# First products of the key/value compression: three rounded passes over two sequences at once, page rows in another order

## What is computed

```python
def compress(kv, pe, w1, w2):                      # kv: (B, L, 2, groups, 64)
    nch = L // 16                                  # 64 chunks of 16 rows
    ch = kv.reshape(B, nch, 16, 2, 2, 64)
    h = einsum('cld,cldh->ch', pe, w1b)            # position term
    for r in range(2):                             # a window is 32 rows: two chunks
        u = einsum('bnscgd,csdh->bncgh', ch, w1r[:, r])
        h = h + u[:, r:r + nch - 1]
    return einsum('bncgh,chd->bncgd', gelu(h), w2)
```

## Time and profile before

| | |
|---|---|
| median of 3 runs | 2172.89 us (2168.56 to 2173.81) |
| profiled execution | 2165.8 us |
| span of its profile, first to last instruction | 2164.2 us |
| mean granted TensorE clock | 0.918 of full |
| busy share PE / PEld / DVE / ACT / POOL | 87% / 73% / 49% / 39% / 9% |

### The profile page before, as it was taken

One profiled execution on the slowest core, in us unless ns is written; L12 is line 12 of the kernel. 1 busy time (PEld: TensorE's weight loads), 2 busy tenths in 40 slices (PEclk: granted clock), 3 DMA queues, 4 the chain that ended last, 5 costly groups with the idle time before them and its releaser, 6 DMA issues. The chain is left out here.

```text
span 2164.2 us, 26795 instructions
## 1 busy us (share of the span) xinstructions
PE 1879.3 (87%) x9820; PEld 1589.7 (73%) x9820; DVE 1059.8 (49%) x1953; ACT 841.7 (39%) x1706; POOL 186.4 (9%) x336
## 2 busy tenths in 40 slices
PE   5996975678888997959948997799999999999997
PEld 4895863457667775738737872699998999989996
DVE  3532345536777875455334441454445544455444
ACT  4311222225666665232034531443333433344443
POOL 0001102103333321010000000000000000000000
PEclk8998987776899998969968998799999999999999
DMA  5414404210000002140022002434333433344341
GB/s 189 182 37 104 115 1 126 89 37 1 1 1 1 1 1 73 54 163 8 1 90 78 1 16 82 137 125 142 122 116 135 162 123 117 119 161 157 138 154 63
DMA packets 109977, 185.21 MB, mean 86 GB/s; under 512 B 18416, under 2 KB 79280, under 8 KB 109799
## 3 DMA queue, kind: packets, MB, share of 16 engines
q1 hardware_dynamic: 89759, 156.84, 21.3%
q0 software_dynamic: 8144, 25.40, 3.6%
q10 hardware_dynamic: 11968, 1.58, 0.6%
HBM read 175.30 MB, written 12.73 MB: 87 GB/s over the span
## 5 line engine op out<-in xcount | busy, mean ns | idle before, releaser
L2428 DVE TENSOR_TENSOR mlp_dn_lo<-mlp_dn_raw,mlp_dn_hi 128x1024 fp32r<-128x1024 f32 x96 | 117.6, 1225 | 299.5 <-ACT mlp_dn_hi L2351 299.5
L2268 PE MATMUL mlp_psU<-mlp_xT_hi,mlp_up_hi 128*128 128x384 f32 (+1 forms) x768 | 254.0, 331 | 5.3 <-DVE mlp_up_lo L2422 5.3
L2268 PE MATMUL mlp_psU<-mlp_xT_hi,mlp_up_lo 128*128 128x384 f32 (+1 forms) x768 | 252.2, 328 | 0.0
L2268 PE MATMUL mlp_psU<-mlp_xT_lo,mlp_up_hi 128*128 128x384 f32 (+1 forms) x768 | 252.1, 328 | 0.0
L2351 ACT CAST mlp_dn_hi<-mlp_dn_raw 128x1024 fp32r<-128x1024 f32 x96 | 100.6, 1047 | 267.3 <-PE mlp_acc L2290 187.4
L2290 PE MATMUL mlp_acc<-mlp_dn_hi,mlp_h_hi 128*128 128x512 f32 x512 | 199.4, 389 | 0.0
L2290 PE MATMUL mlp_acc<-mlp_dn_hi,mlp_h_lo 128*128 128x512 f32 x512 | 199.2, 389 | 0.0
L2290 PE MATMUL mlp_acc<-mlp_dn_lo,mlp_h_hi 128*128 128x512 f32 x512 | 199.2, 389 | 0.0
L2268 PEld LDWEIGHTS mlp_psU<-mlp_xT_hi,mlp_up_hi 128*128 128x128 f32 x768 | 145.1, 189 | 9.4 <-issue 3.3
L2268 PEld LDWEIGHTS mlp_psU<-mlp_xT_lo,mlp_up_hi 128*128 128x128 f32 x768 | 145.2, 189 | 3.1
L2268 PEld LDWEIGHTS mlp_psU<-mlp_xT_hi,mlp_up_lo 128*128 128x128 f32 x768 | 145.0, 189 | 0.0
(11 more groups left out here) (412 smaller groups left out, 4078.3 us busy)
## 6 DMA issues: line engine op xcount, KB each, us to landing
mlp_up_raw<-in_w_up SPq DMA_DIRECT2D x48, 1024.0 KB
...
```

The lines of the kernel that those rows point to most:

```text
L2268: m = nc.tensor.matmul(psU[n % 2][:, 0:w], a[:, u % 2, c, :], b[:, g % 2, c, 0:w], start=(c == 0 and n_pass == 0), stop=(c == KC - 1 and n ...
L2428: nc.vector.tensor_tensor(dn_lo[:, u % 2], dn_raw[:, k, a, :], dn_hi[:, u % 2].bitcast(F32), ALU.subtract).then_inc(s_dl, 1)
```

## The change

- The first products use the same scheme as the other large products of this kernel: operands are split into a rounded part (`hi`) and the rounded rest (`lo`), and hi x hi, hi x lo and lo x hi are accumulated. ACT's copy of each transposed tile now writes `rT_hi`, and DVE subtracts it from the PSUM tile to get `rT_lo`. The weights are split once, by two ACT copies and two DVE subtractions.
- Products run over two sequences at once (`batches`: 0 and 1, 2 and 3, ..., and 8 alone), with 256 columns.
- The rows of a page are loaded in another order: partition 8j+m of a page holds rows 16m+2j and 16m+2j+1. The transfers have the same number of pieces and the same 2 KB each. The columns of one product are then runs of eight adjacent floats. The prompt's rows come by eight transfers.
- DVE's pairing copy k of the next sequence comes right after the subtraction of tile k of this one; `paired` holds one sequence.
- z and the gelu steps come two, three and four sequences behind the tiles (`LATE` = 2). `z` is a ring of four.
- PE's order is: transposes of both next sequences, then the product of the two. A tile of `psT` is free once its subtraction is done. The position term comes after the product of the first two sequences.
- `aT` is allocated after `compress`.

```diff
@@ -460,20 +460,24 @@
     pairs = PAGE // 2
     n_j = STRIDE // 2
     RAW = 3
+    LATE = 2
     with ExitStack() as ctx:
         ph = Phase(nc, ctx, "cmp")
         raw = ph.sb("raw", [P, RAW, 4, 2, 2 * NG, HD])
-        paired = ph.sb("paired", [P, 2, 4, 2 * NG, 2, HD])
-        rT = ph.sb("rT", [P, 2, 2 * NG, 4 * P])
+        paired = ph.sb("paired", [P, 4, 2 * NG, 2, HD])
+        rT_hi = ph.sb("rT_hi", [P, 2, 2 * NG, 2, 4 * P], F32R)
+        rT_lo = ph.sb("rT_lo", [P, 2, 2 * NG, 2, 4 * P], F32R)
         w1 = ph.sb("w1", [P, 2, n_j, 2, HD])
+        w1_hi = ph.sb("w1_hi", [P, 2, n_j, 2 * HD], F32R)
+        w1_lo = ph.sb("w1_lo", [P, 2, n_j, 2 * HD], F32R)
         w2 = ph.sb("w2", [HD, 2, 2 * HD])
         pe_t = ph.sb("pe_t", [P, 2, 2 * n_j])
         pe_b = ph.sb("pe_b", [HD, 2])
         late = ph.sb("late", [HD, 2, NG, NCMP])
-        z = ph.sb("z", [HD, 2, n_seq, NG, NCH])
+        z = ph.sb("z", [HD, 2, 4, NG, NCH])
         z3 = ph.sb("z3", [HD, 2, n_seq, NG, NCH])
         psT = [ph.ps(f"psT{k}", [P, 4, P]) for k in range(2)]
-        psU = [ph.ps(f"psU{k}", [P, 2, NG, NCH]) for k in range(2)]
+        psU = [ph.ps(f"psU{k}", [P, 2, NG, 2, NCH]) for k in range(2)]
...
-        cache = t["cache_cmp_kv"][0].rearrange("n (p r) u g d -> n p (r u g d)", r=2)
-        own = o["p_cmp_kv"][0, 0].rearrange("(k p r) u g d -> p k (r u g d)", p=P, r=2)
+        cache = t["cache_cmp_kv"][0].rearrange("n (m j r) u g d -> n j m (r u g d)", j=n_j, r=2)
+        own = o["p_cmp_kv"][0, 0].rearrange("(k h m j r) u g d -> k h j m (r u g d)", h=2, j=n_j, r=2, m=pairs // n_j)
+        batches = [range(a, min(a + 2, n_seq)) for a in range(0, n_seq, 2)]
         with nc.Block() as block:

-            def load_pages(eng, first, queue_sem):
-
-                for q in range(DB):
+            def load_pages(eng, first, queue_sem, qs):
+
+                for q in qs:
                     if q >= RAW:
                         eng.wait_ge(s_pair, 4 * (q - RAW + 1))
                     for n in range(first, PAST // PAGE, 2):
                         page = eng.value_load(table[0:1, q * DB + n:q * DB + n + 1], min_val=0,
                                               max_val=cache.shape[0] - 1)
                         dst = raw[pairs * (n % 2):pairs * (n % 2) + pairs, q % RAW, n // 2].rearrange("p r c d -> p (r c d)")
-                        eng.dma_start(dst, cache[bass.DynSlice(page, 1)].rearrange("a p f -> (a p) f")
+                        eng.dma_start(dst, cache[bass.DynSlice(page, 1)].rearrange("a j m f -> (a j) m f")
                                       ).then_inc(queue_sem[q % RAW], 16)

             @block.sync
             def _(sp):
-                load_pages(sp, 0, s_raw)
+                load_pages(sp, 0, s_raw, range(DB))
                 sp.wait_ge(s_pair, 4 * (DB - RAW + 1))
                 sp.wait_ge(s_stored, 16 * n_stored)
-                sp.dma_start(raw[:, DB % RAW].rearrange("p k r c d -> p k (r c d)"), own).then_inc(s_raw[DB % RAW], 16)
+                for n in range(PAST // PAGE):
+                    dst = raw[pairs * (n % 2):pairs * (n % 2) + pairs, DB % RAW, n // 2].rearrange("p r c d -> p (r c d)")
+                    sp.dma_start(dst, own[n // 2, n % 2]).then_inc(s_raw[DB % RAW], 16)

             @block.gpsimd
             def _(pool):
-                load_pages(pool, 1, s_raw_odd)
+                load_pages(pool, 1, s_raw_odd, range(DB))

             @block.tensor
             def _(pe):
                 def transposes(q):
                     for k in range(4):
-                        pe.wait_ge(s_pair, 4 * q + k + 1)
                         u = 4 * q + k
+                        pe.wait_ge(s_pair, u + 1)
                         if u >= 2:
-                            pe.wait_ge(s_rT, u - 1)
+                            pe.wait_ge(s_rl, u - 1)
                         for cg in range(2 * NG):
-                            m = nc.tensor.transpose(psT[u % 2][:, cg, :], paired[:, q % 2, k, cg].rearrange("p r d -> p (r d)"),
-                                                    ident[:, :])
+                            m = nc.tensor.transpose(psT[u % 2][:, cg, :], paired[:, k, cg].rearrange("p r d -> p (r d)"), ident[:, :])
                         m.then_inc(s_tr, 1)

                 transposes(0)
                 pe.wait_ge(s_c, 16 * 8)
-                for q in range(n_seq):
-                    if q + 1 < n_seq:
-                        transposes(q + 1)
-                    if q == 1:
+                for v, qs in enumerate(batches):
+                    for q in qs:
+                        if q + 1 < n_seq:
+                            transposes(q + 1)
+                    pe.wait_ge(s_rl, 4 * (qs[-1] + 1))
+                    pe.wait_ge(s_wl, 2)
+                    if v >= 2:
+                        pe.wait_ge(s_z, batches[v - 2][-1] + 1)
+                    for c in range(2):
+                        for j in range(n_j):
+                            for n_pass, (a, b) in enumerate(((w1_hi, rT_hi), (w1_hi, rT_lo), (w1_lo, rT_hi))):
+                                mov = b[:, v % 2, NG * c:NG * c + NG, 0:len(qs), :].rearrange("p g q (x j m) -> p j g (q x) m", j=n_j, m=8)
+                                m = nc.tensor.matmul(psU[v % 2][:, c, :, 0:len(qs), :], a[:, c, j, :], mov[:, j],
+                                                     start=(j == 0 and n_pass == 0), stop=(j == n_j - 1 and n_pass == 2))
+                    m.then_inc(s_u, 1)
+                    if v == 0:
                         pe.wait_ge(s_pl, 32)
                         for c in range(2):
                             for k in range(2 * n_j):
                                 m = nc.tensor.matmul(psE[:, c:c + 1], w1[:, c, k % n_j, k // n_j, :], pe_t[:, c, k:k + 1],
                                                      start=(k == 0), stop=(k == 2 * n_j - 1))
                         m.then_inc(s_pe, 1)
-                    pe.wait_ge(s_rT, 4 * (q + 1))
-                    if q >= 2:
-                        pe.wait_ge(s_z, q - 1)
-                    for c in range(2):
-                        for j in range(n_j):
-                            mov = rT[:, q % 2, NG * c:NG * c + NG, :].rearrange("p g (n j) -> p j g n", j=n_j)[:, j]
-                            m = nc.tensor.matmul(psU[q % 2][:, c, :, :], w1[:, c, j, :, :].rearrange("p r h -> p (r h)"),
-                                                 mov, start=(j == 0), stop=(j == n_j - 1))
-                    m.then_inc(s_u, 1)
                 pe.wait_ge(s_ge, n_seq)
...
+                act.wait_ge(s_c, 16 * 8)
+                for c in range(2):
+                    nc.scalar.copy(w1_hi[:, c, :, :], w1[:, c, :, :, :].rearrange("p j r h -> p j (r h)")).then_inc(s_wh, 1)
+
                 def late_half(act, q):

-                    act.wait_ge(s_u, q + 1)
+                    act.wait_ge(s_u, q // 2 + 1)
                     if q:
                         act.wait_ge(s_z, q)
                     for c in range(2):
-                        m = nc.scalar.copy(late[:, c, :, :], psU[q % 2][HD:P, c, :, 1:NCH])
+                        m = nc.scalar.copy(late[:, c, :, :], psU[q // 2 % 2][HD:P, c, :, q % 2, 1:NCH])
                     m.then_inc(s_late, 1)

-                for q in range(n_seq + 3):
+                for q in range(n_seq + LATE + 2):
                     if q < n_seq:
                         for k in range(4):
                             u = 4 * q + k
                             act.wait_ge(s_tr, u + 1)
-                            if q >= 2:
-                                act.wait_ge(s_u, q - 1)
-                            nc.scalar.copy(rT[:, q % 2, :, k * P:(k + 1) * P], psT[u % 2][:, :, :]).then_inc(s_rT, 1)
-                    if 0 <= q - 1 < n_seq:
-                        late_half(act, q - 1)
-                    if 0 <= q - 2 < n_seq:
-                        act.wait_ge(s_z, q - 1)
-                        nc.scalar.activation(z3[:, :, q - 2], z[:, :, q - 2], ACT.Square).then_inc(s_sq, 1)
-                    if 0 <= q - 3 < n_seq:
-                        act.wait_ge(s_cu, q - 2)
-                        nc.scalar.activation(z3[:, :, q - 3], z3[:, :, q - 3], ACT.Exp,
+                            if q >= 4:
+                                act.wait_ge(s_u, q // 2 - 1)
+                            nc.scalar.copy(rT_hi[:, q // 2 % 2, :, q % 2, k * P:(k + 1) * P], psT[u % 2][:, :, :]).then_inc(s_rh, 1)
+                    if 0 <= q - LATE < n_seq:
+                        late_half(act, q - LATE)
+                    if 0 <= q - LATE - 1 < n_seq:
+                        p = q - LATE - 1
+                        act.wait_ge(s_z, p + 1)
+                        nc.scalar.activation(z3[:, :, p], z[:, :, p % 4], ACT.Square).then_inc(s_sq, 1)
+                    if 0 <= q - LATE - 2 < n_seq:
+                        p = q - LATE - 2
+                        act.wait_ge(s_cu, p + 1)
```

(75 more changed lines are left out.)

5 lines of the change are left out of this document (4 added, 1 removed).

## The result

The changed kernel takes 2175.92 us (median of 20 runs), the kernel before 2168.43 (20 runs): ratio 1.0037, 95% interval 1.0024 to 1.0050. It is slower by 7.5 us, where 2.3 us less was forecast. The forecast time was 2170.6 us, from a median before of 2172.9.

What follows compares the result with a forecast made beforehand. TensorE bounds the kernel before; after the change, the product of two sequences stands in series with DVE's work. Second products move from 317.6 to 315.3, -2.3 us, so 2172.9 becomes 2170.6 us; range 2159 to 2181.

Steps and rivals of the forecast that it cites:

- P(0): First product of two sequences in `compress` (P is such a product): forecast to start at 224.9 us.
- Start: Beginning of `compress`: first tile copy at 210.2, first subtraction 211.6, sequence 1's pages at 212.36 as now.
- the rounds: Repeating work of two sequences in `compress`: 19.85 us at full clock, 22.0 with the low clock.
- T: Start of the second products, at the end of `compress`: forecast 315.3 us, before 317.64.
- the clock: TensorE in `compress`: clock falls to 1.2 GHz every round and P begins low, 19.85 becoming 22.0 us a round.
- P in series with DVE: In each `compress` round, P and DVE's work wait for each other; 9.9 us a sequence at full clock against 10.41.
- the late half: Part of P's result that ACT moves in 0.42 us; DVE waits for it 4 to 6 us once in two sequences.
- The passing of tiles: Transposed tiles going PE-ACT-DVE-PE in `compress`: about 0.25 us for three hand-overs a pass.
- rival (c): Passing of tiles costs more: each 0.5 us a pass adds 1 us a sequence, +7 us, 2180; chance 0.15.
- the pitch: Time per record of the rounded first products: 0.119 us, making 5.7 us for two sequences.
- Rival (b): First products' records take 0.24 us, P 5.8 us longer, four times on the path: +21 us, 2194; chance 0.10.

Runs made afterwards that it cites:

- run 6: Changed kernel with z and the gelu steps one sequence later (`LATE` = 3 for 2): 2165.48 us, ratio 0.9990 to the kernel before.
- Run 7: Changed kernel plus 20 unused rounded products on TensorE after the second tile of each sequence from the fourth on: 2171.65 us, ratio 1.0018 to the kernel before.
- run 8: Changed kernel with products reading 64 adjacent columns (wrong ones) of each tile, not eight runs of eight: 2171.27 us, ratio 1.0015 to the kernel before.
- Run 4: Changed kernel with the old page loads; ACT and DVE write the transposed tiles in the new order: 2164.97 us, ratio 0.9987 to the kernel before.
- Run 9: Kernel before with page rows cut 16 x 4 and products reading columns in the order that undoes this: 2140.77 us, ratio 0.9878.
- run 3: Changed kernel with the position term's loads issued by SP after its first twelve page loads: 2176.89 us, ratio 1.0046 to the kernel before.
- 11: Changed kernel with the position term loaded as 16 whole rows that TensorE transposes: 2172.21 us, ratio 1.0021 to the kernel before.
- run 1: Changed kernel with the old order of page rows, products stepping over eight floats again: 2178.77 us, ratio 1.0053 to the kernel before.
- Run 2: Kernel before with only the new row order (loads cut 8 x 8), no rounding or batches: 2144.44 us, ratio 0.9895.
- 5: Kernel before, loads untouched, with ACT's copy writing the transposed tiles in the new order: 2142.47 us, ratio 0.9872.
- 12: Changed kernel with old page loads, order made by the copies, `LATE` = 3, position term as whole rows: 2157.87 us, ratio 0.9944 to the kernel before.
- 10: Kernel before with ACT's copy writing the new order and the position term as 16 whole rows transposed by TensorE: 2129.74 us, ratio 0.9816.

## Why the prediction was wrong

| step | forecast | measured |
|---|---|---|
| ACT's first copy of a tile | 210.2 | 218.62 |
| first subtraction of a tile | 211.6 | 220.08 |
| P(0) | 224.9 | 232.94 |
| P(1) | 246.2 | 253.62 |
| P(2), P(3) | 268.2, 290.2 | 276.57, 298.99 |
| second products | 315.3 | 324.17 |

**The failed step is "Start".** The prediction took from the kernel before when ACT's queue is done and when the pages land (212.36 for sequence 1), while the change gives each page load another shape. (The row it read as ACT's weight loads, until 207.6, is that of the position term's two loads.) It had the new order of the rows at no cost on the way in: the loads have as many pieces of the same size, and that was all it looked at. In its place the runs show 1.9 us a page load on SP's queue for 1.2, the first pages at 212.18 for 206.90, and 13.99 us for the term's loads on ACT's queue for 5.35. P(0) was forecast for 224.9 and started at 232.94, 8.0 us late. Of these, 7.4 stand between 213.5 and the third tile's transposes at 220.91, the rest in the passes. The 8.9 us at the end are this and 0.9 net from the rounds. About 1 us of it is this one trace: runs 6, 7 and 8 have the same start, and P(0) there is at 231.88, 231.89 and 231.72. Run 4 shows it by taking the new loads away: P(0) at 223.60, T at 316.84, and no loss is left (nor a gain, since its rounds take 2.8 us more than forecast). Run 9 narrows what about the loads does it to the cut in eight (or the distance of the pieces that comes with it). Runs 3 and 11 show the two ways in which it reaches P(0): ACT's queue first, and right behind it the pages themselves.

The measured 2175.92 us lie inside the stated range, 2159 to 2181. That is luck: the range was made for the clock and for the hand-overs between engines, and nothing in it stood for the page loads at the start.

**Right: P in series with DVE.** PE waits for subtractions and DVE for the late half, as said, and run 6 takes the wait away and 3 us a round with it, by the order of work and not by its amount. The passing of tiles was sized right too, so rival (c) did not come: two passes take 2.58 us at the low clock (transposes at 220.91, 223.49, 226.07), 2.68 was forecast.

**Right: the clock.** It falls in every round and P begins low. Run 7 prices it at 2.1 us in the round that is at full clock throughout; 2.2 was forecast. The pattern that the prediction cited from the Trainium skill's page "TensorE: Matmul & The Clock Gate" (section on HAM oscillation), bursts between idle gaps that start at the low clock, is what the trace shows, 0.50 from 265.40 to 279.00.

**Nearly right: the pitch.** 0.119 was forecast, the full-clock value is 0.136, and 0.120 with long rows (run 8). At full clock this is 48 x 0.017 = 0.8 us a P. P took 7.4 to 7.9 us, where 5.7+1.5 = 7.2 was forecast. That may be part of why the rounds take 22.42 to 22.95 in place of 22.0, but it isn't shown: run 8 has the quick pitch and its rounds after P(1), 23.38 and 21.18 us, are on average 0.4 shorter while the one before is 1.3 longer. Rival (b) did not come: its bad end is real, but for single floats (0.218, run 1).

**Missed: what the saving came from.** The prediction credited the quick product to the rounded passes, 5.7 us for two sequences against 14.9. Run 2 shows that the plain fp32 products take 7.31 us for two sequences once their columns lie in runs of eight. P takes 7.4 to 7.9 in the changed kernel (253.62 to 261.06, 276.57 to 284.43), and 6.87 us at full clock (run 7). So rounding saves 0.4 us for two sequences at best, and nothing at the clock it gets. With it come 2.4 us of subtractions a sequence, P in DVE's loop and the falling clock. Together with the batches and the order of work it costs 22.5 us between runs 4 and 5, and 28 between 12 and 10; what rounding alone costs of this is not shown. The whole gain lay in the order of the columns that a product reads.

What stays open: why slower page loads also hold up ACT's loads of single floats, beyond that both go with the cut in eight (runs 2 and 9). In run 3, where SP issues the same two loads behind its twelve page loads, they take 4.17 us, so it isn't the cut alone. Open too is what about the later phases makes up the rest of the 7 us in the profiled pair, once the two executions' distance from their medians is taken off.
